# From the output projection to the experts: barriers, the norm, the shared expert and the slot lists

## The reference, cut to what matters

```
xl = xl + mod_l[2] * (mix_l @ w_out[l])
hl = modulate(rms_norm(xl, norm2_g[l]), mod_l[3], mod_l[4])     # layer 0: the context tokens too
scores = sigmoid(h @ router_w)
_, idx = top_k(scores + router_bias, 6)                         # 64 experts, 6 for each token
gates = scores[idx] / sum(scores[idx]) * 2.5
y = sum over the 6 of gate * swiglu(h, w_gu[e], w_down[e]) + swiglu(h, shared_gu, shared_down)
xl = xl + mod_l[5] * y
```

## Time and profile before

| | us |
|---|---|
| median of 3 runs | 3123.18 |
| the profiled execution | 3120.62 |
| its span, first to last instruction | 3118.8 |
| PE busy | 2425.7 (78%) |
| DVE busy | 793.9 (25%) |
| ACT busy | 423.4 (14%) |
| POOL busy | 316.8 (10%) |

### The profile page before, as it was taken

The page is one execution under the profiler, slowest core; times in us unless marked ns, Lnnn a source line. Parts: engine busy times, 40 slices in busy tenths (PEclk is TensorE's granted clock), DMA queues, the critical chain, the costliest instruction groups (busy, mean ns, idle before and its releaser), DMA issues. The chain is left out here.

```text
span 3118.8 us, 36476 instructions
## 1 busy us (share of the span) xinstructions
PE 2425.7 (78%) x15075; PEld 1329.5 (43%) x15075; DVE 793.9 (25%) x1515; ACT 423.4 (14%) x850; POOL 316.8 (10%) x374
## 2 busy tenths in 40 slices
PE   5979869967599889888880797929668888888883
PEld 2448625444244444444440356826423343434341
DVE  1224555224011111111114413564321011101112
ACT  1022224210000000000000203224100000000000
POOL 0015100003111101011100004300020101010100
PEclk8989969878799999999995898969779999999996
DMA  6100175231599999999966110001379999999992
GB/s 257 36 37 3 69 273 201 72 133 63 216 424 425 421 413 403 398 401 396 396 248 250 47 45 2 9 2 55 120 294 424 422 419 419 415 418 408 413 395 110
DMA packets 123194, 775.93 MB, mean 249 GB/s; under 512 B 34904, under 2 KB 45288, under 8 KB 66832
## 3 DMA queue, kind: packets, MB, share of 16 engines
q1 hardware_dynamic: 99984, 735.70, 58.3%
q0 software_dynamic: 23040, 37.82, 3.3%
HBM read 770.93 MB, written 44.44 MB: 261 GB/s over the span
## 5 line engine op out<-in xcount | busy, mean ns | idle before, releaser
L1310 PE MATMUL banks<-arena,htreg 128*64 128x384 f32 (+1 forms) x4096 | 826.7, 510 | 119.8 <-DMA arena<-in_exp_w_gu 116.9
L1310 PEld LDWEIGHTS banks<-arena,htreg 128*64 128x64 f32 (+1 forms) x4096 | 406.0, 151 | 551.8 <-issue 366.7
L1328 PE MATMUL banks<-arena,modreg 128*64 128x512 f32 (+1 forms) x1536 | 414.4, 617 | 72.8 <-DMA arena<-in_exp_w_down 45.6
L1982 DVE TENSOR_TENSOR modreg<-modreg,banks 128x384 f32<-128x384 f32 x74 | 41.0, 555 | 929.3 <-ACT modreg L1533 929.3
L1328 PEld LDWEIGHTS banks<-arena,modreg 128*64 128x64 f32 (+1 forms) x1536 | 154.5, 150 | 282.7 <-issue 282.7
L2166 POOL DMA_INDIRECT y_d<-modreg,lst x74 | 75.6, 1021 | 1398.2 <-DVE modreg L1988 1398.2
L950 PE MATMUL banks<-arena,htreg 128*128 128x428 f32 x512 | 184.2, 522 | 0.0
L1988 DVE COPY modreg<-banks 128x512 f32<-128x512 f32 x74 | 51.2, 692 | 448.0 <-PE banks L1328 448.0
L1533 ACT ACTIVATE modreg<-banks 128x384 f32<-128x384 f32 x74 | 36.3, 490 | 947.8 <-PE banks L1310 947.8
L950 PEld LDWEIGHTS banks<-arena,htreg 128*128 128x128 f32 x512 | 97.5, 190 | 86.7 <-issue 86.7
L904 PE MATMUL banks<-const,hreg 128*128 128x128 f32 x112 | 23.8, 388 | 139.2 <-DVE hreg L1598 139.2
(11 more groups left out here) (349 smaller groups left out, 2437.3 us busy)
## 6 DMA issues: line engine op xcount, KB each, us to landing
arena<-in_exp_w_gu SPq DMA_DIRECT2D x256, 1536.0 KB, 27.0
arena<-in_exp_w_down SPq DMA_DIRECT2D x128, 1536.0 KB, 27.3
modreg<-in_w_mod SPq DMA_DIRECT2D x40, 1024.0 KB, 5.0
arena<-y_d SPq DMA_DIRECT2D x6, 3072.0 KB, 17.7
arena<-in_w_in SPq DMA_DIRECT2D x8, 1712.0 KB, 10.7
modreg<-mod_d SPq DMA_DIRECT2D x20, 512.0 KB, 7.0
arena<-in_w_out SPq DMA_DIRECT2D x2, 4096.0 KB, 13.0
arena<-in_w_mod SPq DMA_DIRECT2D x6, 1024.0 KB, 9.7
```

The source lines that it names most:

```text
L1310: last = mm(ps[2 + half][rows, 0:DE], hgT[n % 2][:, k, rows], up4[q][:, i, DE * half:DE * (half + 1)], start=(k == 0), stop=(k == KD - 1))
L1328: last = mm(ps[4 + half][rows, :], actT[:, k, rows], dn3[q][:, k, 512 * half:512 * half + 512], start=(k == 0), stop=(k == KE - 1))
```

## The change

- The barriers behind the projection, behind the norm and behind the shared expert are gone.
- Norm by tile: square, root, scale and shift, transposes and router products of a tile follow its projection. On PE the order is projection i, transposes i-1, router i-2. Modulation rows, router weights and the shared expert's weights are loaded before.
- The shared expert's weights are the first three chunks of the ring, slots 0 to 2, and its tiles the first units (`NSH`, 4 and 2) of the same loop. The ring has 8 slots. Slot 0 is given back when the last shared unit has used it. Scratch moves behind the ring and over the modulation rows, and one row set is loaded again later.
- The lists of the units' slots are made on the chip: ranks by a product with ones, a one-hot slot row times a code for each tile and choice (DVE), multiplied by the one-hot expert rows and summed on PE, then by a one-hot of the unit. Gates and the addresses of the lists in memory come later on DVE; POOL's 24 and 12 scatters of codes stand one behind each unit from the third on.
- Priming uses slot 7 of the ring and starts when `h` is stored; SP waits for it only before it fills slot 7.

```diff
 UNITS = tuple((NE + w) // 2 for w in WHOLE)
 CHUNK = 3072
-SLOTS = 9
-FIRST_SLOT = 3
+SLOTS = 8
...
+NSH = NOUT
+WORK = [[(None, (i,)) for i in range(NSH[l])] + work(l) for l in LAYERS]
...
-CHUNKS = [[(n, part, j) for n, (_, ranks) in enumerate(WORK[l]) for part in PARTS for j in range(len(ranks))]
-          for l in LAYERS]
-SLOT_OF = [{c: (i + FIRST_SLOT) % SLOTS for i, c in enumerate(CHUNKS[l])} for l in LAYERS]
+CHUNKS = [[(n, part, j) for n, (_, ranks) in enumerate(WORK[l]) if n == 0 or n >= NSH[l]
+           for part in PARTS for j in range(len(ranks))] for l in LAYERS]
+SLOT_OF = [{c: i % SLOTS for i, c in enumerate(CHUNKS[l])} for l in LAYERS]
...
-        phase_end(sp, "sp")
-        load_mod(l, 1)
-        sp.dma_start(rw[:], router_w[l].rearrange("(k p) n -> p k n", p=P)).then_inc(router_loaded.sem, 16)
-        sp.dma_start(sgu, shared_w_gu[l].rearrange("(k p) n -> p k n", p=P)).then_inc(shared_loaded.sem, 16)
-        sp.dma_start(sdn, shared_w_down[l].rearrange("(k p) n -> p k n", p=P)).then_inc(shared_loaded.sem, 16)
+        load_mod(l, 1, range(2))
+        for part in range(2):
+            sp.dma_start(up4[part], shared_w_gu[l].rearrange("(k p) n -> p k n", p=P)[:, 4 * part:4 * part + 4, :]
+                         ).then_inc(chunk_loaded[part].sem, 16)
+        sp.dma_start(chunk[2], shared_w_down[l].rearrange("(p k) n -> p (k n)", p=P)).then_inc(chunk_loaded[2].sem, 16)
+        sp.wait_ge(nocode_ready.sem, nocode_ready.at(l, 1))
+        sp.dma_start(list_d.rearrange("(p a) b -> p (a b)", p=P), nocode).then_inc(lists_cleared.sem, 16)
...
-        sp.wait_ge(h_stored.sem, h_stored.at(l, NOUT[l]))
-        phase_end(sp, "sp")
-        sp.wait_ge(nocode_ready.sem, nocode_ready.at(l, 1))
-        sp.dma_start(list_d.rearrange("(p a) b -> p (a b)", p=P), nocode).then_inc(lists_cleared.sem, 16)
+
+        load_mod(l, 1, [2])
...
-        loaded = 0
+        loaded = len(PARTS)
         for n, (_, ranks) in enumerate(WORK[l]):
+            if n < NSH[l]:
+                continue
...
-                    if loaded == SLOTS - FIRST_SLOT - 3:
-
-                        sp.wait_ge(listed.sem, listed.at(l, TOPK * NOUT[l]))
...
-                        phase_end(sp, "sp")
                     if loaded >= SLOTS:
 
                         m, was, _ = CHUNKS[l][loaded - SLOTS]
+                        m = max(m, NSH[l] - 1)
                         sp.wait_ge(free_by[was].sem, free_by[was].at(l, m + 1))
+                    if loaded == SLOTS - 1:
+
+                        sp.wait_ge(primed.sem, 1)
                     load_chunk((n, part, j), experts)
                     loaded += 1
+        sp.wait_ge(listed.sem, listed.at(l, TOPK * NOUT[l]))
+        sp.dma_start(lst[:, 0:R[l], :], list_d[LIST1:LIST1 + LIST2].rearrange(
+            "(r s e) b -> s r (e b)", s=P, e=NE)[:, 0:R[l], :]).then_inc(lists_loaded.sem, 16)
...
-        phase_end(pe, "pe")
-        norm(2 * l + 1, OUT_TILES[l])
...
+        def normed(i):
+            t = OUT_TILES[l][i]
+            pe.wait_ge(h_ready.sem, h_ready.at(u, i + 1))
+            for half in range(2):
+                n = 2 * i + half
+                if n >= 2:
+                    pe.wait_ge(hT_ready.sem, hT_ready.at(u, n - 1))
+                for k in range(4):
+                    last = pe.transpose(ps[4 + n % 2][:, tok(k)], h[:, t, tok(4 * half + k)], ident)
+                last.then_inc(hT_psum.sem, 1)
...
+        for i in range(n_t + 2):
+            if i < n_t:
+                projected(i)
+            if 1 <= i <= n_t:
+                normed(i - 1)
             if i >= 2:
+                routed(i - 2)
+
+        def positions():
+            pe.wait_ge(mask_ready.sem, mask_ready.at(l, 1))
+            end = NE * (n_t + 1)
+            last = mm(ps[1][:, 0:end], K("str_b"), mask[:, 0:n_t + 1, :].rearrange("p t e -> p (t e)"), start=True, stop=False)
+            for j in range(n_t):
+                last = mm(ps[1][:, NE * (j + 1):end].rearrange("p (t e) -> p t e", e=NE), ones, bc(mask[:, j, :], 1, n_t - j),
+                          start=False, stop=(j == n_t - 1))
+            last.then_inc(pos_psum.sem, 1)
+
+        def ranks():
+            pe.wait_ge(beats_ready.sem, beats_ready.at(l, 1))
+            mm(ps[0][:, 0:NE], ones[0:NE, :], beats[0:NE, :], start=True, stop=True).then_inc(rank_psum.sem, 1)
+
+        def lists_by_expert():
+            for m in range(TOPK * n_t):
+                i, k = divmod(m, TOPK)
+                pe.wait_ge(slot_hot_ready.sem, slot_hot_ready.at(l, m + 1))
+                last = mm(ps[1][0:NE, 0:P], onehot[:, i, k, :], slot_hot[:, m % 4, :], start=(m == 0), stop=(m == TOPK * n_t - 1))
+                last.then_inc(slot_hot_used.sem, 1)
+
+        def lists_by_unit():
+            pe.wait_ge(listT_ready.sem, listT_ready.at(l, 1))
+            mm(ps[0][:, 0:UNITS[l]], listT, unit_hot[0:NE, 0:UNITS[l]], start=True, stop=True).then_inc(list_psum.sem, 1)
...
+        def unit_up(n, between=None):
+            if n >= NSH[l]:
+                pe.wait_ge(slotT.sem, slotT.at(l, n - NSH[l] + 1))
+                src = hgT[(n - NSH[l]) % 2]
+            else:
+                src = hT[:, :, tok(OUT_TILES[l][n])]
             if n:
                 pe.wait_ge(unit_act.sem, unit_act.at(l, n))
+            else:
+                pe.wait_ge(resid_ready.sem, resid_ready.at(l, 2 * n_t))
...
+        unit_up(0, between=positions if n_t == 2 else None)
+        if n_t > 2:
+            positions()
+        unit_down(0)
+        ranks()
+        unit_up(1)
+        lists_by_expert()
+        unit_down(1)
+        lists_by_unit()
+        for n in range(2, NSH[l]):
+            unit_up(n)
+            unit_down(n)
+        unit_transposed(NSH[l])
+        for n in range(NSH[l], NW[l]):
...
-        phase_end(act, "act")
-        norm(2 * l + 1, OUT_TILES[l])
-        phase_end(act, "act")
+        u = 2 * l + 1
+        for i, t in enumerate(OUT_TILES[l]):
+            act.wait_ge(resid_ready.sem, resid_ready.at(l, 2 * i + 2))
+            fn(h[:, t, :], xs[:, t, :], ACT.Square, accum_out=stat[:, i:i + 1]).then_inc(squares_ready.sem, 1)
+            act.wait_ge(meansq_ready.sem, meansq_ready.at(u, i + 1))
+            fn(stat[:, 8 + i:9 + i], stat[:, 4 + i:5 + i], ACT.Sqrt).then_inc(std_ready.sem, 1)
+            for half in range(2):
+                act.wait_ge(hT_psum.sem, hT_psum.at(u, 2 * i + half + 1))
+                fn(hT[:, 4 * half:4 * half + 4, tok(t)], ps[4 + half].rearrange("p (k n) -> p k n", k=4),
+                   ACT.Copy).then_inc(hT_ready.sem, 1)
...
-        phase_end(dve, "dve")
-        norm(2 * l + 1, OUT_TILES[l])
-        phase_end(dve, "dve")
-
+            u, sd = 2 * l + 1, t // 2
+            dve.wait_ge(squares_ready.sem, squares_ready.at(u, i + 1))
+            ts(stat[:, 4 + i:5 + i], stat[:, i:i + 1], 1.0 / D, EPS, ALU.mult, ALU.add).then_inc(meansq_ready.sem, 1)
+            dve.wait_ge(std_ready.sem, std_ready.at(u, i + 1))
+            link(dve.reciprocal(stat[:, 12 + i:13 + i], stat[:, 8 + i:9 + i]))
+            if i == 0:
+                dve.wait_ge(mod_loaded.sem, mod_loaded.at(u, 4))
+            link(stt(h[:, t, :], xs[:, t, :], stat[:, 12 + i:13 + i], mod[:, 1, sd, :], ALU.mult, ALU.mult))
+            tt(h[:, t, :], h[:, t, :], mod[:, 0, sd, :], ALU.add).then_inc(h_ready.sem, 1)
...
-            link(tt(onehot[i], bc(K("experts"), 1, TOPK), bc(idxf[:, i, 0:TOPK], 2, NE), ALU.is_equal))
-            link(red(mask[:, i, :], onehot[i].rearrange("p k e -> p e k"), AX, ALU.add))
-            link(tt(ohp, onehot[i], bc(scores[:, i, :], 1, TOPK), ALU.mult))
-            link(red(gate[:, i, 0:TOPK], ohp, AX, ALU.add))
-        dve.nop().then_inc(mask_ready.sem, 1)
-        link(red(gatesum[:, 0:n_t], gate[:, 0:n_t, 0:TOPK], AX, ALU.add))
-        link(dve.reciprocal(gatesum[:, 0:n_t], gatesum[:, 0:n_t]))
-        link(stt(gate[:, 0:n_t, 0:TOPK], gate[:, 0:n_t, 0:TOPK], ROUTED, bc(gatesum[:, 0:n_t], 2, TOPK),
-                 ALU.mult, ALU.mult))
+            link(tt(onehot[:, i], bc(K("experts"), 1, TOPK), bc(idxf[:, i, 0:TOPK], 2, NE), ALU.is_equal))
+            ins = red(mask[:, i, :], onehot[:, i].rearrange("p k e -> p e k"), AX, ALU.add)
+            if i < n_t - 1:
+                link(ins)
+            else:
+                ins.then_inc(mask_ready.sem, 1)
+        if n_t > 2:
+            unit_times(0)
+
...
+        link(tt(row64, key, ident[:, 0:NE], ALU.mult))
+        link(red(keycol, row64, AX, ALU.add))
+        ts(beats[lo64], key[lo64], keycol[lo64], None, ALU.is_lt).then_inc(beats_ready.sem, 1)
+        link(ts(row64[lo64], key[lo64], keycol[lo64], None, ALU.is_gt))
+        link(red(rankcol[lo64], row64[lo64], AX, ALU.add))
+        link(ts(dropcol[lo64], rankcol[lo64], float(U_), float(U_ - W_), ALU.is_ge, ALU.mult))
+        link(tt(rankcol[lo64], rankcol[lo64], dropcol[lo64], ALU.subtract))
```

(50 more changed lines are left out.)

347 lines of the change are left out of this document (166 added, 181 removed).

## The result

The changed kernel takes 3031.99 us, the median of 4 runs (3030.5 to 3033.8), the kernel before on the same chip 3121.23 (3117.06 to 3123.61): a ratio of 0.9716 with a 95% interval of 0.9699 to 0.9733. 89 us are gained where 98 were forecast, and the time lies 7 us above the 3025 of the prediction (the kernel before is 2 us faster here than the 3123.2 from which it was counted). The profiled execution took 3032.81 us, its span is 3030.9.

The account below looks back on a forecast made before the run. Two long expert-weight streams and what delays them were taken to bound the kernel. Gains of 69 us in layer 0 and 30 in layer 1, less 1 for scatters, made 98 off 3120.6: 3022.6, as a median 3025 us, range 3002 to 3064.

Parts of the forecast that it names:

- (1): Layer 0 projection: with transposes and a tile's router products now in between, its end moves from 651.0 to 654.0.
- (2): Layer 0 norm and router: barrier and load waits leave the path; sigmoid ends at 668.0 instead of 698.6, 31 us less.
- (3): Layer 0 mask and counting: mask 8.8 us instead of 13.5; counting, behind the first shared gate-up, ends at 679.5.
- (4): Layer 0 sort and first weight issue: issue at 691.0, 37 us sooner; priming takes some 27 us, hidden.
- (5): Layer 0 shared units set the pace: 24 comparisons at 0.32 us; down 1 ends at 714.0, down 3 at 750.3.
- (6): Layer 0 gathers and addresses: DVE's addresses are late, not gathers; first routed gate-up at 761.4 instead of 833.6, 72 sooner.
- (7): Layer 0 ring turnover with 8 slots: one transfer, 3.8 us, lost; tenth chunk at 773.2 instead of 841.8; 69 us gained.
- Layer 1: Two tiles, no priming: first routed gate-up at 2275.7 instead of 2308.1, tenth chunk at 2287.8 instead of 2317.5; 30 us gained.
- (a): Rival, shared units of both layers: comparisons cost 0.7 us each and PE runs slow; 33 us less gain, 3058; chance 0.15.
- (b): Rival, layer 0 stream: one slot less banks one chunk fewer, missed in some eight groups; 30 us, 3055; chance 0.07.
- (d): Rival, both streams: landing time is latency, so fewer slots lower the rate; 256 us longer, 3281; chance 0.05.
- (c): Rival, list scatters inside the streams: each holds the DMA engines for 2.2 us; 79 us in all, 3104; chance 0.05.

Follow-up runs that it names:

- e6: The kernel before without POOL's four priming DMAs in layer 0: 3098.73 us, ratio 0.9934.
- e2: The changed kernel with DVE computing the list addresses behind the copy of the first routed unit's slots, not ahead of it: 3019.88 us, ratio 0.9691.
- e0: The changed kernel run again with nothing altered, as the measure for the others: 3030.85 us, ratio 0.9723.
- e4: The changed kernel with seven ring slots instead of eight: 3038.53 us, ratio 0.9743.
- e5: The changed kernel without POOL's list scatters and without the overflow path's lists: 3030.9 us, ratio 0.9709.
- e1: The changed kernel with the router weights loaded late, after the attention phase, in both layers: 3015.62 us, ratio 0.9676.
- e7: The kernel before with the router weights loaded early, right behind the output weights: 3131.97 us, ratio 1.0038.
- e10: The changed kernel with the norm grouped (all tiles projected, then normed, then routed) instead of by tile: 3043.66 us, ratio 0.9766.
- e11: The changed kernel with one barrier put back between shared and routed units in both layers: 3053.0 us, ratio 0.9803.
- e8: The changed kernel with router load late, addresses late and, in layer 1 only, the lists made sooner: 2999.1 us, ratio 0.9624.
- e3: The changed kernel with both the router load late and the addresses late: 3006.65 us, ratio 0.9639.

## Why the prediction was right, and where it was off

The mechanism is as forecast, nearly step by step: what stands ahead of each stream shrinks, and the streams keep their rate. Counted in us from the start of the projection's matmuls, forecast and measured in layer 0:

| step | forecast | measured |
|---|---|---|
| (1) projection ends | 58 | 58.5 |
| (2) sigmoid ends | 72 | 73.8 |
| (3) positions on PE | 84 | 87.6 |
| (4) first weight issue | 95 | 99.0 |
| (5) down 1 ends | 118 | 118.3 |
| (5) down 3 ends | 154 | 156.8 |
| (6) first routed gate-up | 165.5 | 167.3 |

- **(2)** One term was too small, the router products with 1.7 us. The prediction reads the 64 rows of before as 64 products, of which a tile has 8; each product is two rows in the trace (x16 for a tile, x32 for two), so a tile takes 3.5 us at the slow clock. And two tiles' products, not one's, stand behind the last transposes: 6.93 us. That the step is only 1.8 us off is luck: other terms were too large by some 3.5. ACT loads a table once ahead of the first Sqrt (1.28 us) and not again between the tiles, as taken. The same miscount is in (3), where 5 products are set against 28 rows of 14 products; they took 1.9 us for 1.5.
- **(3), (4)** The first shared gate-up began at 681.73 and took 12.7 us, so counting came later. The first weight issue is 4 us late by it. That was hidden: the five free slots are not needed until the shared units are through.
- **(4)** Priming's four DMAs were issued within 10 us (676.61 to 686.19), not 27. Before, they shared the queue with six weight chunks; here no weights move. Off the path either way; e6 puts what it cost before at 20.6.
- **(5)** The comparisons, which no row of before showed, took 0.26 us each (0.32 taken, between 0.23 and 0.7), one group of 24 on DVE:

```profile
713.51 6.24 DVE L2009 TENSOR_SCALAR arena<-const,arena 128x128 f32<-128x128 f32 x24
```

- **(6)** DVE's addresses are what is late next, as said: e2 took them away and gained 11.
- **(7), the ring:** at most one transfer a layer. Layer 0 gives 70.4 - 4.0 = 66.4 where 69 were forecast. From nine to eight slots the first stream is 4.0 us longer (1.4 in e0), the second not at all; from eight to seven each is longer by one transfer (e4).
- **Layer 1:** 35.3 + 1.0 = 36.3 where 30 were forecast. The gathers land in 8.9 us instead of 10, and the 3.8 us of the shorter ring are not lost there: the second stream is no longer than it was. Why the ninth slot was worth nothing in this layer, no run shows.
- **The scatters:** nothing that can be measured (e5), 1 us forecast.

**The step that failed** is none of the seven. It is the early router load, which the prediction names as leaving the path behind the norm and prices at nothing where it goes to. Putting it in front of SP's chain of modulation pieces costs 12.7 us in the trace, 15 by e1 and 12.6 by e7. With it at its old place the changed kernel gains 102.7 us (94 to 108 by the interval of e1), which holds the 98 forecast. What stands behind it in SP's queue there, and what that feeds, was never asked. That the whole is only 9 us short is in part luck: the 12.7 us lost there and 2.6 in layer 0 met 6.3 more than forecast in layer 1.

Of the rivals, (a) did not come: only the first shared gate-up is slow (12.7 us), those after it take 10.5 and not 13.1, and the comparisons took 0.26 and not 0.7. (b) and (d) fell with the unchanged rate of the streams and with e4, (c) with e5.

**The gain by parts,** as far as runs took them apart: priming 20.6 (e6), norm by tile 13 (e10), the barrier before the routed units 22 (e11), the early router load -13 to -15 (e1, e7). What is left of the 89, 46 to 48, is the rest by difference: the two barriers behind projection and norm with the loads that stood between them, the lists made on the chip, and the shared weights in the ring. They were not tried alone, and parts that share a wait need not add.

## What to carry to other kernels

Where a saturated stream ends the kernel, count everything up to the point where its buffers turn over; each microsecond there is one at the end (e11), and a buffer beyond saturation is worth at most one transfer (e4, and nothing in the second stream from nine to eight). A small load that is moved earlier is not free: look at what stands behind it in its queue, and whether an engine whose clock reacts to waits is fed by that. Work that nobody waits for, such as the addresses here, belongs behind the copy that everybody waits for.

## What the hardware showed that I had not expected

- With 1 us more of waiting on PE the clock stayed at 1.2 GHz for 17 us instead of 7, which cost 4.3 us, and in nine of nine profiles a second stretch grew from 14 to 31 us, which cost 8.3. The length of this phase takes few values, not a continuum: from the first wait to the projection it is 135.9 to 136.4 us in four profiles, 144.2 in e8, and 148.8 to 149.9 in nine.
- A load of 1024 rows of 256 B behind 4 MB made SP need 8.7 us to issue the next two stores, one of 128 rows of 2 KB 1.12. The time of the kernel was the same.
- The same gate-up took 10.5, 12.2 or 13.4 us, with a mean clock of 1.00 in e2 and 0.78 in the changed kernel, and the length of the wait ahead of it does not say which (1.4 us before both 10.54 in e2 and 13.52 in e3).
